# Four layers on one core: values centred as they are turned, merges by whole transposes, new order tables in layer one, and decay rates made beside layer two's output

## What is computed

```python
# layer one, 16 heads of 64
kk = heads(k * k_k)
kk = kk / jnp.maximum(jnp.sqrt(jnp.sum(kk * kk, axis=-1, keepdims=True)), 1e-12)
k = k * (1.0 + (a - 1.0) * k_a)
def rwkv7_step(state, inp):
    r_t, w_t, k_t, v_t, kk_t, a_t = inp
    sa = jnp.einsum('bhvk,bhk->bhv', state, -kk_t)
    state = state * w_t[:, :, None, :] + sa[..., None] * (kk_t * a_t)[:, :, None, :] + v_t[..., None] * k_t[:, :, None, :]
    return state, jnp.einsum('bhvk,bhk->bhv', state, r_t)
mu = jnp.mean(y, axis=-1, keepdims=True)                  # over a head
var = jnp.mean(jnp.square(y - mu), axis=-1, keepdims=True)
y = ((y - mu) * lax.rsqrt(var + GN_EPS)) * lnx_w + lnx_b + bonus
# layer three
log_a = -LRU_C * r * jax.nn.softplus(-a_param)            # the decay rate
a = jnp.exp(log_a); mult = jnp.sqrt(-jnp.expm1(2.0 * log_a))
```

## Time and profile before

| what | value |
|---|---|
| median of 3 runs | 1917.3 us (1914.47 to 1918.16) |
| profiled execution | 1917.06 us |
| its span, first to last instruction | 1915.3 us |
| mean granted TensorE clock | 0.97 |
| layer one, about | 50 to 702 us |
| its output | 702 to 818 us |
| layer two and its output | 818 to 1327 us |
| layer three and its output | 1327 to 1581 us |
| layer four and its output | 1581 to 1915 us |

### The profile page before, as it was taken

One profiled execution on the slowest core, in us unless ns is written; L12 is line 12 of the kernel. 1 busy time (PEld: TensorE's weight loads), 2 busy tenths in 40 slices (PEclk: granted clock), 3 DMA queues, 4 the chain that ended last, 5 costly groups with the idle time before them and its releaser, 6 DMA issues.

```text
span 1915.3 us, 33665 instructions
## 1 busy us (share of the span) xinstructions
PE 1764.4 (92%) x13616; PEld 1313.6 (69%) x13616; DVE 1314.2 (69%) x2382; ACT 784.9 (41%) x1454; POOL 803.2 (42%) x719
## 2 busy tenths in 40 slices
PE   5999999999999959999889999898799898899987
PEld 5677777777776647765766666586577676677756
DVE  7689999999998756247996565524787617155553
ACT  3424324324333352355334344433477523244442
POOL 3534334334333234556862111343355554444433
PEclk9999999999999989989999999998899898999998
DMA  7312212212212123211221011021322130433312
GB/s 280 96 50 92 88 46 89 90 46 84 95 46 90 68 69 104 97 58 64 88 68 50 29 42 34 24 97 44 110 78 82 58 106 30 152 126 121 103 50 88
DMA packets 51882, 154.80 MB, mean 81 GB/s; under 512 B 5888, under 2 KB 12032, under 8 KB 51600
## 3 DMA queue, kind: packets, MB, share of 16 engines
q1 hardware_dynamic: 51728, 152.65, 23.9%
HBM read 150.50 MB, written 2.13 MB: 80 GB/s over the span
## 4 chain that ended last, share of the span: by engine, by line
PE 67%; DVE 22%; ACT 5%; issue 2%; DMA 1%; POOL 1%; SPq 0%; DVEq 0%; ACTq 0%; POOLq 0%
PE bank L498 16%; PE bank L500 15%; PE bank L499 15%; PE bank L1206 6%; DVE ya L1517 4%; PE bank L2171 3%; PE bank L2159 2%; PE bank L2193 2%; DVE tables L1427 1%; PE bank L2556 1%; PE bank L2796 1%; DVE score L2288 1%; DVE best L2285 1%; PE bank L2811 1%; DVE h_lo L972 1%
## 5 line engine op out<-in xcount | busy, mean ns | idle before, releaser
L481 POOL TENSOR_TENSOR w_lo<-raw,w_hi 128x512 fp32r<-128x512 f32 (+2 forms) x434 | 560.3, 1311 | 801.8 <-ACT w_hi L463 801.8
L498 PE MATMUL bank<-h_hi,w_hi 128*128 128x512 f32 x1368 | 594.5, 435 | 59.7 <-POOL h_lo L1009 27.5
L500 PE MATMUL bank<-h_hi,w_lo 128*128 128x512 f32 x1368 | 543.1, 397 | 0.0
L499 PE MATMUL bank<-h_lo,w_hi 128*128 128x512 f32 x1368 | 542.0, 396 | 0.0
L498 PEld LDWEIGHTS bank<-h_hi,w_hi 128*128 128x128 f32 x1368 | 261.9, 191 | 161.0 <-issue 94.7
L463 ACT ACTIVATE w_hi<-raw 128x512 fp32r<-128x512 f32 (+2 forms) x434 | 241.6, 600 | 305.1 <-PE bank L500 226.8
L499 PEld LDWEIGHTS bank<-h_lo,w_hi 128*128 128x128 f32 x1368 | 262.8, 192 | 59.5 <-issue 15.5
L500 PEld LDWEIGHTS bank<-h_hi,w_lo 128*128 128x128 f32 x1368 | 261.4, 191 | 58.9
L1517 DVE SCALAR_TENSOR_TENSOR ya<-padded,vecs,ya 128x512 f32<-128x512 f32 x240 | 200.1, 834 | 1.7
L2228 ACT ACTIVATE probs<-probs,small 128x512 f32<-128x512 f32 x64 | 46.3, 724 | 109.0 <-DVE small L2211 108.6
L2865 DVE CUSTOM_DVE_ANT_0 fox_probs<-bank,fox_keybias 128x128 f32<-128x128 f32 (+3 forms) x64 | 28.8, 488 | 84.5 <-PE bank L2796 84.3
(11 more groups left out here) (392 smaller groups left out, 2906.9 us busy)
## 6 DMA issues: line engine op xcount, KB each, us to landing
raw<-even_in SPq DMA_DIRECT2D x57, 512.0 KB, 3.6
raw<-odd_in SPq DMA_DIRECT2D x39, 512.0 KB, 3.5
raw<-ada SPq DMA_DIRECT2D x32, 512.0 KB, 3.5
raw<-fox_in SPq DMA_DIRECT2D x25, 512.0 KB, 3.5
raw<-lru_in SPq DMA_DIRECT2D x24, 512.0 KB, 3.5
ada_first<-ada SPq DMA_DIRECT2D x16, 512.0 KB, 13.8
raw<-even_out SPq DMA_DIRECT2D x16, 512.0 KB, 3.5
raw<-odd_out SPq DMA_DIRECT2D x16, 512.0 KB, 3.4
```

Source lines behind the costliest of these rows:

```text
L481: e.tensor_tensor(k.w_lo[s % NSPLIT][:, at], k.raw[n % NRAW][:, at], k.w_hi[s % NSPLIT][:, at].bitcast(F32), ALU.subtract).then_inc(*did(" ...
L498: e.matmul(out, hi[:, w], x[i][0], start=start and i == 0, stop=False, skip_group_check=True)
L499: e.matmul(out, hi[:, w], x[i][1], start=False, stop=False, skip_group_check=True)
L500: m = e.matmul(out, lo[:, w], x[i][0], start=False, stop=stop and i == kt - 1, skip_group_check=True)
```

## The change

It does these things:
- the values are transposed by a product with `centring` (identity less 1/64 within a head), so that y comes out centred; `f_sum` and `f_centre` go;
- both inverse roots are made on ScalarE as Exp(-0.5 Ln(..)); the eight reciprocals of VectorE per block go, scale factors are folded into neighbouring operations (halved biases and taps, `(tanh + 1)` in place of the sigmoid's own pass);
- `off` and `merge` work on crossed halves with two banks, `turn` is four 128x128 transposes; ScalarE copies `off` in two halves and VectorE adds `merge` in two halves;
- new order tables for all four engines;
- the decay rates of layer three are made beside layer two's output;
- the first six results of layer three are split inside the layer.

```diff
+        self.centring = sb("centring", [P, P])
...
+    e.scalar_tensor_tensor(k.centring[:, :], k.head_ones[:, :], -1.0 / RH, k.ident[:, :], ALU.mult, ALU.add).then_inc(
+        *did("made", "centring"))
...
             for c in range(TT):
-                m = e.transpose(bank[:, c * P:(c + 1) * P], two(src(c)), k.ident[:, :])
+                if name == "V":
+                    m = mul(bank[:, c * P:(c + 1) * P], two(src(c)), k.centring[:, :])
+                else:
+                    m = e.transpose(bank[:, c * P:(c + 1) * P], two(src(c)), k.ident[:, :])
...
+        crossed = [(h * TT // 2 + c // 2, h, c, g) for h in range(2) for c in range(TT) for g in range(2)]
...
-            four(("off", m), p, w[3 - 2 * m], PT, ("activated", "off", p, m), ("pooled", "off", p, m), done)
+            bank, free = banks(("off", m), p, 2, ("activated", "off", p, m, 0), ("activated", "off", p, m, 1))
+            wait(*free, ("pooled", "off", p, m), done)
+            for n, h, c, g in crossed:
+                t = mul(bank[g][HALVES[c % 2][1], at_chunk(n)], w[3 - 2 * m][HALVES[g][1], h, c, :], PT[HALVES[g][1], h, c, :])
...
-            for n in range(2 * TT):
-                h, c = divmod(n, TT)
-                for g, gs in HALVES:
-                    t = mul(bank[gs, at_chunk(n)], PT[gs, h, c, :], k.ident[gs, gs])
+            for n in range(TT):
+                h, c = divmod(2 * n, TT)
+                t = e.transpose(bank[:, n * P:(n + 1) * P], PT[:, h, c:c + 2, :].rearrange("p c t -> p (c t)"), k.ident[:, :])
...
-            four(("merge", m), p, w[0], w[2], ("made", "merged", p, m), ("made", "turned", p, m), ("activated", "off", p, m))
+            for n, h, c, g in crossed:
+                on = HALVES[c % 2][1]
+                t = mul(bank[c % 2][HALVES[g][1], at_chunk(n)], w[0][on, h, c - c % 2 + g, :], w[2][on, h, c - c % 2 + g, :])
...
-        e.activation(sq, k.bank.get(("kk_sum", q)), ACT.Sqrt).then_inc(*did("activated", "kk_root", q))
+        e.activation(buf, k.bank.get(("kk_sum", q)), ACT.Relu, bias=k.minus_least).then_inc(*did("activated", "kk_over", q))
+        e.activation(buf, buf, ACT.Ln, bias=k.least).then_inc(*did("activated", "kk_log", q))
+        e.activation(buf, buf, ACT.Exp, scale=-0.5).then_inc(*did("activated", "kk_root", q))
...
-        e.activation(b, k.bank.get(("f_sum2", p)), ACT.Sqrt, bias=k.gn_eps, scale=1.0 / RH).then_inc(
-            *did("activated", "f_root", p))
+        e.activation(b, k.bank.get(("f_sum2", p)), ACT.Ln, bias=k.gn_eps, scale=1.0 / RH).then_inc(
+            *did("activated", "f_log", p))
+        e.activation(b, b, ACT.Exp, scale=-0.5).then_inc(*did("activated", "f_root", p))
...
-    return ["f_sum", "f_centre", "f_square", "f_sum2", "f_root", ("f_inv", 0), ("f_inv", 1), ("f_inv", 2), ("f_inv", 3),
-            "f_norm", "f_out"]
+    return ["f_square", "f_sum2", "f_root", "f_norm", "f_out"]
```

The middle cycle's table, TensorE's and the end of VectorE's, and ScalarE's last one:

```diff
 ORDER = {
     "tensor": """
-        w_up val2' val3' k0 val4' mm0 U' val5' val6' Y' tA k1 y' bonus_sum' tV val7' k2 k3 k4 k5 k6 k7 f_sum gate0'
-        gate1' gate2' gate3' gate4' mm1 N gate5' r0 r1 a_up gate6' gate7' f_sum2 Z tK r2 tB sq1 r3 r4 sq2 sq2p sq3
-        sq3p r5 r6 sq4 r7 v0 off0 turn0 kk_sum v1 merge0 v2 v3 off1 turn1 v4 v5 merge1 v6 v7 PAt U0 PA G C glu0 glu1
-        chain1 glu2 glu3 glu4 chain2 glu5 chain3 glu6 glu7 chain4 chain5 val0 val1 chain6""",
+        w_up tA mm0 val6' val7' tV bonus_sum' f_sum2 a_up gate0' gate1' gate2' k0 mm1 k1 N gate3' gate4' gate5' gate6'
+        gate7' k2 k3 k4 k5 k6 k7 sq1 Z tK tB sq2 r0 sq2p sq3 sq3p r1 r2 sq4 kk_sum off0 turn0 r3 r4 r5 r6 merge0 r7 v0
+        off1 turn1 v1 v2 v3 merge1 v4 v5 v6 v7 PAt U0 PA G C glu0 glu1 chain1 glu2 chain2 glu3 chain3 glu4 chain4 glu5
+        glu6 glu7 val0 chain5 val1 chain6 val2 val3 val4 U Y val5 y""",
...
+        ada1 turn1 tap11 kk_norm tap12 tap13 tap14 merge1 tap15 tap16 PAt tap17 G C tap18 chain1 tap19 chain2 tap20
+        chain3 A chain4 B chain5 ada2 chain6 tap21 r_lerp tap22 U R rk v_lerp tap23 ada3""",
...
 LAST_ORDER = {
     "scalar": """
-        PA wcg11 wcg20 wcg21 cg_done2 centre0 centre1 centre2 centre3 centre4 centre5 centre6 centre7 ln_root cg_done3
-        wcg30 wcg31 wcg40 wcg41 ln0 cg_done4 cg_done5 wcg50 ln1 ln2 wcg51 wcg60 wcg61 cg_done6 cg_done7 ln3 ln4 ln5
-        wcg70 wcg71 t1 ln6 ln7""",
+        centre2 centre3 centre4 centre5 centre6 centre7 ln_root wcg21 wcg30 wcg31 t1 cg_done3 wcg40 wcg41 ln0 ln1
+        cg_done4 wcg50 cg_done5 ln2 ln3 ln4 wcg51 wcg60 cg_done6 ln5 ln6 wcg61 wcg70 wcg71 cg_done7 ln7""",
```

Layer three:

```diff
+def lru_rates_vector(k, e, need, did):
+    yield 3.0
+    e.tensor_copy(rate[:, 0, :], k.vec("lru_a", 0, LT)).then_inc(*did("made", "lru_a"))
+    yield 5.0
+    softplus_of_minus(e, need, did, "lru_softplus", rate[:, 0, :], aux[:, 0, :], aux[:, 1, :], aux[:, 2, :], [])
...
+            pairs, sq = self.out_buffers(LT, inner)
+            self.lru_out = pairs[LT // 2:] + pairs[:LT // 2], sq
...
+    def early():
+        for n in range(LT // 2):
+            yield n + 2.2
+            own_high(e, need, did, "lru", n, k.lru_out[0], lambda i: k.Y[:, i, :], lru_y_ready(n))
```

291 lines of the change are left out of this document (153 added, 138 removed).

## The result

The changed kernel takes 1870.79 us (median of 4 runs, 1867.37 to 1872.26) against 1917.73 (4 runs, 1914.47 to 1918.41): ratio 0.9758, 95% interval 0.9742 to 0.9775, 46.9 us faster. The forecast was 1860.7, in a range of 1844 to 1878. The profiled execution took 1871.9 us, its span 1870.2.

The account below looks back on a forecast made before the run. TensorE and VectorE both nearly fill layer one's cycles; with VectorE relieved, TensorE's work is the only floor. 19.5 + 2.3 + 5.2 + 7.8 + 4.9 + 9.7 + 7.0 = 56.4 us off 1917.06 gives 1860.7 us, range 1844 to 1878.

Parts of the forecast that it names:

- The cycles: Layer one's six middle cycles: crossing, turns and the dropped head sum, less centring, save 3.25 us each, 19.5 us together.
- The new order tables: Layer one's cycles: fewer runs of projection chunks, costed at nothing because the waits they could take are small.
- near 59 us: Sign to look for: VectorE's busy time per cycle of layer one, 69.5 us before, falls near 59 us.
- Rival 1: Layer one's cycles: the tight order makes TensorE wait 1.5 to 2 us more each; 14 us back, 1875 us, chance 0.2.
- The last block (5.2), with the first (2.3): Layer one: last block saves 3.25 us plus 2 of idle; first solved block, with no first sum to lose, saves 2.3.
- edge: End of layer one: tanh behind row six cuts the wait before the output from 14.1 to 6.3 us, saving 7.8.
- Layer one's output: ScalarE squares directly, so the second head sum starts 4.9 us earlier; the later weight wait neither adds nor pays.
- Layer three's head: Moving the decay rates starts the gates 8.1 us earlier; with the clock regained, 9.7 us, bounds 6 and 11.
- The sign that I gave: Layer three's gates: TensorE's wait falls under 2 us and is released by the gates' DMA.
- Layer three's output: Early splits remove TensorE's 7.54 us wait and keep its clock; the twelfth result gives about 2 back; 7 us saved.
- ScalarE's roots: Layer one's cycles: roots by Ln and Exp stay hidden; one table by the skill page, two more loads as bound.
- Rival 5: Layer one's blocks: a late root holds the head sum's bank, with some 2.8 us slack; slower, 1925 us, chance 0.02.

Follow-up runs that it names:

- u4: Changed kernel with corrections and merges as straight 64x64 products and turns of 64x64, as before the change; 1887.04 us (ratio 0.9851).
- x4: Changed kernel with only the turns as 16 products of 64x64 again, corrections and merges still crossed; 1878.71 us (ratio 0.9791).
- u1: Changed kernel with the order tables of the kernel before and all the new arithmetic; 1883.99 us (ratio 0.9834).
- x2: Changed kernel with every GpSimd weight split cut to 16 columns, leaving most weights' rests out of the computation; 1834.19 us (ratio 0.9556).
- v3: Changed kernel with four names moved in the last order table, on TensorE, ScalarE and VectorE; 1866.96 us (ratio 0.9736).
- u2: Changed kernel with the decay rates made at layer three's head again; 1876.90 us (ratio 0.9789).
- u3: Changed kernel without the early splits of layer three's first six results; 1870.89 us (ratio 0.9765).
- v2: Changed kernel with one projection chunk moved ahead of the second squarings in TensorE's middle table; 1867.42 us (ratio 0.9741).

## Why the prediction was right, and where it was not

The direction, the range and most mechanisms stood; the gain was 47 us where the sum said 56.4. Stage by stage the span got shorter by 27.7 us up to layer one's output (34.8 forecast), 8.1 in that output (4.9), 7.7 at layer three's head (9.7), 1.8 in layer three and its output (7.0) and 1.4 in layer four (nothing forecast); layer two took 1.4 us more. Together that is the 45.1 us between the two profiled spans. By step, from the two profiled executions:

- **The cycles (19.5 us): right.** The mean over six kernels with that code is 20.6 (432.7 less 412.1), 18.8 in the changed kernel's own trace. The terms were right to 0.1 us: crossing 1.84 a cycle, measured 1.77 (u4 less x4, undisturbed cycles); turns 1.0, measured 1.09; centring 0.54, measured 0.48 (0.89 less 0.41). TensorE's busy time per cycle fell from 70.59 to 67.21 us, by 3.4 where the sum has 3.25.
- **"The new order tables I cost at nothing": wrong, and hidden.** By u1 they are worth 1.6 us a cycle. Without them ScalarE's copy and a weight split stop TensorE; with them TensorE still waits 0.9 us in each cycle, and another 1.5 in some. The idle time that I kept, 1.5 us, is 1.5 on average too (68.7 less 67.2), but by other waits than before: that the size came out is luck.
- **VectorE "near 59 us": wrong.** It is 63.7 to 65.0, and 58.7 with GpSimd's splits cut (x2). The count of passes was right; the forecast had no term for two engines that hold each other up. The Trainium skill, page "SBUF — State Buffer", section "Who interferes with whom", states it: the pair of ports that VectorE has beside its own is GpSimd's only one and an exclusive lock, a VectorE instruction with two SBUF inputs contends with a GpSimd instruction that reads SBUF, and the order of issue decides who blocks. The trace agrees, with either engine as the loser: 3.39 for 2.31 us, or 1.66 for 1.29, and at the third tap of 36 cycles the one that starts first wins, but for two splits that start up to 0.05 us after the tap and still hold it.
- **Rival 1, a tight order that stalls**, is there in part: long cycles in three of six places here, ten of 36 over the six kernels. Its place is right (a chain step behind a tap), its price 1.7 us where it strikes, and whether it strikes hangs on shifts of 0.1 to 0.2 us between a tap and a split. My argument against it, that VectorE has slack now, left GpSimd out.
- **The last block (5.2), with the first (2.3): wrong.** The whole of layer one up to the output gained 27.7 us (703.80 to 676.13) where 34.8 were forecast; with the cycles at 18.8, first block, last block and edge gave 8.9 for 15.3. The wait before the output fell to 6.13, as forecast (6.3). But the last table opened two waits of 2.2 us, the values' copy behind f_square and a conv gate behind the normalisation, and TensorE's granted clock, 1.00 before, was 0.50 from 658.8 to 661.9 us, behind the second. The centring behind the first took 2.08 us for 1.05. v3 shows that shifting names wins back 3 us, not 5: the two ends of the block are tied.
- **Layer one's output (4.9): right in its step, low in sum.** The second head sum comes 5.1 us earlier after the output's start (6.38 us for 11.47). But the stage from the output's start to the squares before layer two is 102.9 us for 111.0, 8.1 less, and 100.8 to 105.3 in the other kernels that compute the whole. The later wait, which was to neither add nor pay, fell from 3.25 to 2.71 us, and behind it TensorE's granted clock is 1.00 (707.4 to 714.0) where it was 0.76 (741.8 to 748.0). Which edit brings the rest is not shown.
- **Layer three's head (9.7): the mechanism right, the price 7.67** (u2 gives the same to a hundredth), against 8.1 for the earlier start and 1.65 for the clock. The sign that I gave, a wait under 2 us released by the gates' DMA, did not come: it is 2.94 us, put down to VectorE. Late next was not the load alone: the taps, which I priced at 2.3 us from a trace in which the rates' small steps took GpSimd's four splits upon themselves (1.2 instead of 0.2 us for four of them), now meet those splits and take 5.0. They end within 0.1 us of the load. TensorE's granted clock was 0.50 at the first gates as before (2.07 us), so that part didn't come back either.
- **Layer three's output (7): wrong, 2.2** (u3). The wait of 7.54 us went, as forecast, with 7.0 us; I gave 2 back for the twelfth result, it was 4.8. ScalarE's copies of the next weight stand behind five splits and four activations, so that the weight's rest is 2.54 us late; TensorE's granted clock was then 0.50 from 1474.5 to 1477.5, and it waited 1.46 for the result.
- **Rates beside layer two's output: hidden, as forecast.** Its output lasts 96.93 us with them and 96.95 without (u2).
- **ScalarE's roots: hidden, as forecast, but not the one table.** Ln and Exp load a table each (at 248.72 and 250.75 us in the middle cycle shown), five loads of 1.28 us a cycle in place of four, one more and not the two of my bound. The Trainium skill, page "ScalarE: Activation LUTs", section "Table sets: the hidden batching unit", would have had the pair in one load; the trace disagrees. Rival 5's bank is tighter than I wrote: one chunk fewer between the head sum and the second correction made TensorE wait 0.45 us (v2), so the slack there is about 0.23 us (a chunk's 0.68 less 0.45), not 2.8.

## What to carry to other kernels

When two engines both stream the same on-chip memory, count their passes together: a pass priced from a moment when the other was idle is not its price elsewhere, and whichever engine the change makes quicker will meet the other at a new place. When a wait goes, look for everything that ends within a microsecond of it; here the taps and the load, the weight's rest and the last result, the copy and the gate each stood in pairs, and removing one paid little. Price a group of short products by the distance to the next start only against a group with the same kind of follower; here the difference of the lengths (0.46 us) was right and a distance taken ahead of different followers (0.36) was not.

## What was not expected of the hardware

- One GpSimd split of 128x512 (1.3 us alone) holds a VectorE pass of 0.75 us up to 1.83 us (the longest of 180 taps; their median is 0.748), or is itself stretched to 1.66. Cutting the splits to 16 columns saved 37 us of 1871.
- The same instructions in the same order gave cycles of 68.3 and 70.0 us within one execution (u3), and among 36 cycles of six kernels only those were long that have a pass of 0.16 us over 128x1 ahead of the taps.
- Sixteen crossed products of 64x64 take 0.62 us from start to the start of a projection's chunk where sixteen straight ones take 1.08. In the crossed merges the half of the rows changes only with every second product, in the crossed corrections with each, and both take 0.62. Why is not shown by any run here.
